# RWKV scan: the product with the inverse is issued ahead of the next step's scores

## The reference, cut to what matters

```python
    def step(S, inp):
        rt, wt, kt, vt, at, bt = inp
        sa = jnp.einsum('bhvk,bhk->bhv', S, at)
        S = S * wt[:, :, None, :] + sa[..., None] * bt[:, :, None, :] + vt[..., None] * kt[:, :, None, :]
        return S, jnp.einsum('bhvk,bhk->bhv', S, rt)

    s_fin, y = lax.scan(step, s0.astype(f32), seq, reverse=reverse)
    ...
    y_f, s_f, k_f = direction(0, s0_f, False)
    y_b, s_b, k_b = direction(1, s0_b, True)
    y = y_f + y_b
```

## Time and profile before

| | |
|---|---|
| median of 3 runs | 3835.06 us (3826.1 to 3835.59) |
| the profiled execution | 3833.91 us, its span 3832.1 us |
| PE busy over the span | 3514.5 us, 92% |
| DVE, ACT, POOL busy | 2410.0, 962.5, 1929.7 us |
| the scan's steps | 1334.8 us (first `s_R`) to 1742.2 us (last output copy) from the span's start |

### The profile page before, as it was taken

How to read it: one execution, slowest core, us unless ns; L and a number is a source line. 1 busy time by engine, 2 the same in 40 slices (tenths; PEclk the granted TensorE clock), 3 DMA queues, 4 the chain that set the end, 5 groups by cost and what they waited for, 6 DMA issues and landing times.

```text
span 3832.1 us, 74088 instructions
## 1 busy us (share of the span) xinstructions
PE 3514.5 (92%) x31676; PEld 3298.2 (86%) x31676; DVE 2410.0 (63%) x3150; ACT 962.5 (25%) x1950; POOL 1929.7 (50%) x1067
## 2 busy tenths in 40 slices
PE   6999999999789788889999994799999999999998
PEld 2777899999788678888999994799999777899997
DVE  6355688667884477646784768887586555622125
ACT  5433230001243355532300112300012333310010
POOL 1333556656265656626566651366554333466662
PEclk8999999999899899989999997899999999999999
DMA  8100134333145444332343431244332100122221
GB/s 326 61 18 18 45 106 147 127 116 111 66 152 187 133 91 100 83 92 68 124 138 121 133 95 36 85 141 134 111 124 69 35 18 18 56 78 77 72 77 50
DMA packets 226856, 367.66 MB, mean 96 GB/s; under 512 B 104753, under 2 KB 111089, under 8 KB 226417
## 3 DMA queue, kind: packets, MB, share of 16 engines
q1 hardware_dynamic: 171408, 255.08, 22.2%
q10 hardware_dynamic: 55136, 107.98, 8.1%
HBM read 326.47 MB, written 36.54 MB: 95 GB/s over the span
## 4 chain that ended last, share of the span: by engine, by line
PE 76%; DVE 12%; ACT 3%; issue 2%; DMA 2%; SPq 1%; POOL 1%; ACTq 0%; DVEq 0%; POOLq 0%
PE ps L853 58%; PE ps L1114 3%; PE ps L903 2%; PE ps L1127 2%; PE ps L1145 2%; DVE r_t L2554 1%; PE ps L920 1%; DVE x L2350 1%; DVE r_hlo L2538 1%; PE ps L1086 1%; PE ps L1068 1%; DVE ps L2703 1%; DVE x L2359 1%; DVE m_mx L2482 1%; DVE s_T L2702 1%
## 5 line engine op out<-in xcount | busy, mean ns | idle before, releaser
L680 POOL TENSOR_TENSOR w_hi<-w_raw,zrow 128x1024 fp32r<-128x1024 f32 x354 | 694.5, 1962 | 1237.6 <-PE ps L853 890.4
L682 POOL TENSOR_TENSOR w_lo<-w_raw,w_hi 128x1024 fp32r<-128x1024 f32 x354 | 900.3, 2543 | 27.8
L2252 DVE SCALAR_TENSOR_TENSOR f_acc<-f_unit,silu_c,f_acc 128x512 f32<-128x512 f32 x504 | 630.7, 1292 | 7.6
L853 PE MATMUL ps<-f_hhi,w_hi 128*128 128x320 f32 x2688 | 634.1, 317 | 0.0
L853 PE MATMUL ps<-f_hhi,w_lo 128*128 128x320 f32 x2688 | 613.0, 309 | 0.0
L853 PE MATMUL ps<-f_hlo,w_hi 128*128 128x320 f32 x2688 | 610.8, 308 | 0.0
L853 PEld LDWEIGHTS ps<-f_hlo,w_hi 128*128 128x128 f32 x2688 | 449.6, 188 | 0.0
L853 PEld LDWEIGHTS ps<-f_hhi,w_lo 128*128 128x128 f32 x2688 | 448.9, 188 | 0.0
L853 PEld LDWEIGHTS ps<-f_hhi,w_hi 128*128 128x128 f32 x2688 | 441.2, 188 | 0.0
L853 PE MATMUL ps<-f_ahi,w_hi 128*128 128x320 f32 x1408 | 322.1, 310 | 0.0
L853 PE MATMUL ps<-f_ahi,w_lo 128*128 128x320 f32 x1408 | 320.8, 309 | 0.0
(11 more groups left out here) (399 smaller groups left out, 6714.1 us busy)
## 6 DMA issues: line engine op xcount, KB each, us to landing
w_raw<-in_w SPq DMA_DIRECT2D x340, 512.0 KB, 3.5
f_unit<-in_ada_w ACTq DMA_DIRECT2D x72, 1024.0 KB, 6.0
ada_ring<-in_ada_w SPq DMA_DIRECT2D x24, 1024.0 KB, 6.6
up_scratch<-r_o ACTq DMA_DIRECT2D x40, 320.0 KB, 3.0
s_LW<-up_scratch SPq DMA_DIRECT2D x16, 320.0 KB, 5.0
s_LA<-up_scratch SPq DMA_DIRECT2D x8, 640.0 KB, 7.0
x<-in_x SPq DMA_DIRECT2D x1, 2560.0 KB, 18.0
x_scratch<-r_o ACTq DMA_DIRECT2D x8, 320.0 KB, 2.2
```

The costliest lines, as they stand in the source:

```text
L680: nc.gpsimd.tensor_tensor(whi[:, slot, :], raw[:, raw_slot, :], zrow[:, 0:1].to_broadcast([P, CH * P]), ALU.add).then_inc(w_hi_done, 1)
L682: nc.gpsimd.tensor_tensor(wlo[:, slot, :], raw[:, raw_slot, :], whi[:, slot, :].bitcast(F32), ALU.subtract).then_inc(w_split, 1)
L853: last = mm(ps[:, 2 * b + h, 0:HT], w, r[:, h * HT:(h + 1) * HT], start=kt == 0 and n < 2, stop=kt == KT - 1 and n >= 4)
L2252: last = stt(acc[:, cd, :], unit[:, k, :], by, acc[:, cd, :], ALU.mult, ALU.add)
```

## The change

`scores(*after)` moves from ahead of `solve(i, s)` to behind it. Nothing else is changed; in the last step of all there are no next scores, so 79 of the 80 steps are written differently.

```diff
                         if here:
                             rest_of_state(i, s)
                             output_early(i, s)
-                        if then:
-                            scores(*after)
                         if here:
                             solve(i, s)
                         if then:
+                            scores(*after)
                             turn_keys(*after)
                         slot(i, s, 0)
                         if here:
```

## The result

| | before | changed |
|---|---|---|
| median | 3834.7 us (7 runs, 3826.1 to 3835.6) | 3860.3 us (7 runs, 3847.3 to 3871.8) |
| profiled execution | 3833.9 us | 3858.4 us |

The changed kernel takes 1.007 times as long, 95% interval 1.0059 to 1.0081: 27 us by this ratio, 25.6 us by the medians. The forecast was 3854 us, 19 us slower, with a range of 3843 to 3866.

A forecast was written before the change was run, and what follows sets the result against it. The prediction took PE as the bound, with about 56 us of waits in the scan. Losses by pair summed to 19.3 us, nothing gained, on the profiled 3833.9 us: 3853.2, forecast as median 3854 us, range 3843 to 3866.

The forecast's parts named there:

- An earlier solve gives nothing: At solve, ACT's 82 us of waits are idle time nobody waits for, since state_late never waits for s_U; gain nothing.
- Lost cover, on-time steps: In 49 of 80 steps, where s_R is written about when output_early ends, PE loses 0.12 us a step, 5.9 us raw.
- Lost cover, late steps: In 25 steps where ACT does slot work ahead of s_R, the full 0.67 us is lost, 16.8 us raw.
- the clock: Rival, chance 0.14: longer PE waits in steps 8, 9 and 0 of six pairs bring 1.2 GHz, 11 us more, 3865 us.
- The second term, the mask: From step 5 of pairs 1 to 4, DVE's mask and norms come 1.06 us later, and PE waits for them.
- Weight loads: If the scores' first load went ahead across the waiting solve, some 8 us saved, sum 11; forecast kept 19.
- the sum of 19.3 us: Forecast loss over the scan, added up pair by pair from 0.5 us in pair 0 to 3.4 in pair 1.
- Absorbed: Rival, chance 0.20: later PE waits swallow the losses at steps with late s_R; only 6 to 11 us stay, 3840 to 3846.
- The signs: Expected profile: PE's s_R waits over 60, about 30 us; ACT's solve wait stays; step 5's mask 1 us later; pairs 3 us longer.

The follow-up runs named there:

- undoing step 5: Changed kernel with unread matmuls ahead of solve, but step 5 of pairs 1 to 4 in the old order without them: 3847.8 us, ratio 1.0039 against before.
- the filler: Changed kernel plus unread identity matmuls ahead of solve in steps 5, 6, 8, 9 and 0 of pairs 1 to 4, step 0 of 5 to 7: 3853.3 us, ratio 1.0045.

## Why the prediction was right, and what it sized too low

- *An earlier solve gives nothing.* Right. ACT's 82 us of waiting for `solve` shrank to 50.7 and reappeared ahead of `s_BK`. PE did not wait for `s_U` before and does not now, and delaying `solve` by 0.47 us cost nothing either.
- *Lost cover, on-time steps: 0.12 us each, 49 steps.* Right for the step: pair 3 is 0.36 us longer over steps 1 to 4, just as summed. That the on-time steps alone measured 6.5 us, near the raw 5.9, is partly chance, since 4.0 of the 7.2 us in that profile are pair 0's.
- *Lost cover, late steps: 0.67 us each.* Right: the wait of the row in (3,5) is 1.00 us where it was 0.33, and in (3,9) 2.30 where it was 1.63, each 0.67 more. Alone they cost 23 us with what the clock adds in the median run, and 15.6 us in the scan of the profiled run, whose clock is that of the kernel before; the forecast has 15.7.
- *The second term, the mask.* Right: pairs 1 to 4 take 1.03 to 1.05 us longer from step 5 to step 8, against 1.06 forecast, and undoing step 5 gives back more than its own cover. The attribution was a little too narrow: 0.23 of it comes from step 4's mask.
- *Weight loads.* Keeping 19 in place of 11 was right. In step (3,5) of the changed kernel PEld too takes up `solve` only at 1539.64, and the scores' first load starts at 1539.87: no load went ahead across the wait.
- *What was sized too low.* Two things are missing in the sum of 19.3 us, where the scan of the first profile grew by 26.8 and that of the second by 32.9.

  The first is the clock, to which the forecast gave a chance of 0.14 as a case of its own and nothing in the sum. PE is busy 14 us longer in the first profile and 19 in the second, for the same matmuls. The seven runs of the changed kernel roughly follow it: 3847.3 us at the highest granted clock (0.965), 3866.7 and 3871.8 at the lowest (0.959). The sign that the prediction named for this, a clock clearly under 0.94 over the scan, is there in part: 0.92 and 0.91. Its price in the forecast, 11 us for all six pairs, is of the right order (the filler gives 8 back), but it does not fall on each wait alike, as pairs 1 and 3 in the two profiles show.

  The second is DVE and POOL in each other's way, at which the forecast did not look: it cost 1.8 us in step (0,5) and 1.7 us in step (7,8) beyond what was forecast there (see the last section). This is read from the traces; no edit tested it.

  The two kernels that changed the late and the on-time steps apart ran at the clock of the kernel before, and their scans grew by 15.6 and 7.2 us: about 23 us are there without a lower clock, where the sum has 19.3.
- *The filler* takes 8 us off, with the clock kept up. That it leaves 17 us, near the sum, does not prove the sum: its clock over the scan, 0.96, is above that of the kernel before, and its scan is still 22.0 us longer.
- *A rule on the clock.* In these traces the lower level stands behind a wait of 1.63 us in one pair and not behind one of 2.30 us in another. The Trainium skill, "TensorE: Matmul & The Clock Gate", section "HAM oscillation — how this bites in real kernels", says that idle gaps of PE which are long enough send it back to half rate time and again. The traces agree for the longest gap (0.50 of 2.4 GHz behind 3 us without work); they do not give a length from which on it happens.
- *Absorbed.* Did not happen to the extent of its case. Where the releaser was independent, waits did swallow losses, and in pair 6 all of them, which the forecast did not have: the wait for the DMA at corner V is 2.54 us where it was 4.43.
- *The signs.* PE's wait for the right side came to 29.9 us in all, as forecast (about 30), but in 29 waits and not in over 60: the list counts none in most on-time steps. ACT's wait for `solve` was to stay and fell. The mask in (3,5) starts 1.01 us later against the copy of the right side.

Luck has a part in how near the sum comes, since it is too low in some pairs and too high in another. From one pair's first copy of the right side to the next pair's (in pair 7 to its last), in the first profiles:

| pair | 0 | 1 | 2 | 3 | 4 | 5 | 6 | 7 |
|---|---|---|---|---|---|---|---|---|
| forecast, us | 0.5 | 3.4 | 3.2 | 3.1 | 2.8 | 1.9 | 1.6 | 2.8 |
| measured, us | 2.7 | 3.0 | 3.9 | 4.5 | 4.9 | 3.8 | -0.2 | 4.3 |

Such a row moves by several us from one execution to the next: in the second profile of the changed kernel pair 1 is 9.3 us longer and pair 5 1.5 us shorter.

Left open: why `turn_keys` ahead of `solve` has the lowest clock of all, and what decides from one execution to the next where the lower level falls.

## What to carry to other kernels

An engine's long wait for another says what it waits for, not that anyone is waiting for it: look up who reads its result, and how long that reader is held, before moving work forward. In a list worked through in order, independent work belongs ahead of the instruction that waits, and its worth there is the smaller of its own length and the wait. Count also who takes the moved work's result: here steps 5 to 7 of a pair lost not the sum of their cover but the 1.04 us by which the mask, and DVE's work behind it, came later. And a longer wait can cost more than its length, when PE's clock falls around it.

## What was not expected of the hardware

- Matmuls that nobody reads, put into waits of PE, made a kernel about 8 us faster (ratio 1.0045 for 1.0067 against before); the granted clock over the scan rose from 0.92 to 0.96.
- The lower clock stood around a wait of 2.30 us (0.63 on average over the 9 us from 1562) in some pairs and not in others with the same wait, and it changed places between two profiles of the same kernel.
- The same DVE subtraction of 128x640 elements (L2662, L2663 before) took 1.03 us in step (7,8) before and 2.37 us after the change. The traces show why: it and POOL's instructions do not run at the same time here. In the scan and just behind it, in all 12 profiled executions, it takes 0.80 to 0.82 us where no POOL instruction is under way at its start, and otherwise it ends 0.67 to 0.69 us after that instruction of POOL has ended. Before the change:

```profile
1735.29 2.47 POOL L680 TENSOR_TENSOR w_hi<-w_raw,zrow 128x1024 fp32r<-128x1024 f32 x1
1737.42 1.03 DVE L2663 TENSOR_TENSOR t_hlo<-t_z,t_hhi 128x640 fp32r<-128x640 f32 x1
```

and after it:

```profile
1762.68 2.82 POOL L682 TENSOR_TENSOR w_lo<-w_raw,w_hi 128x1024 fp32r<-128x1024 f32 x1
1763.81 2.37 DVE L2662 TENSOR_TENSOR t_hlo<-t_z,t_hhi 128x640 fp32r<-128x640 f32 x1
```

Before, POOL had 0.34 us left to run; after, the later mask lets DVE begin 1.13 us into POOL's next one, with 1.69 us left. PE then waits 1.71 us ahead of `turned`, where its gap was 0.13, and the step takes 6.22 us for 4.07. It is the place in time that counts, not the new order as such: the two kernels with scores and `turn_keys` ahead of `solve`, in all or in some steps, meet it as well (5.80 and 6.03 us).

- In step (0,5) the prefix scan (two instructions in one row) and POOL take turns in the same way. Before the change DVE begins first, and the scan ends after 4.12 us:

```profile
1363.58 4.12 DVE L2606 TENSOR_TENSOR_SCAN s_PS<-s_keep,s_LW 128x650 f32<-128x650 f32 x2 [3.32 <-DMA s_LA<-up_scratch]
1363.67 2.66 POOL L736 TENSOR_TENSOR s_AR<-s_kk,s_E 128x640 f32<-128x640 f32 x1
```

After it the two start together by the rows; POOL is not held up, and by their lengths each half of the scan comes behind one POOL instruction:

```profile
1364.48 5.53 DVE L2605 TENSOR_TENSOR_SCAN s_PS<-s_keep,s_LW 128x650 f32<-128x650 f32 x2 [3.38 <-DMA s_LA<-up_scratch]
1364.48 1.47 POOL L736 TENSOR_TENSOR s_AR<-s_kk,s_E 128x640 f32<-128x640 f32 x1
1366.02 2.62 POOL L741 TENSOR_TENSOR s_b<-s_kd 128x640 f32<-128x640 f32 x1
```

In both the scan ends 1.37 us after POOL's last instruction beside it (1366.33 and 1368.64). Steps (0,5) to (0,7) take 3.9 us longer. In the eight profiled executions in which DVE does not start first, both of the changed kernel among them, step (0,5) took 13.3 to 15.3 us, and in the four in which it does 11.4 to 11.7. What DVE waits for there is a DMA; why it landed later against POOL's list in each kernel with another order in the on-time steps was not tested.
